# Moving a two-block transformer kernel's buffers by 64 bytes in SBUF, so that weights, 512-token and 256-token activations start at chosen multiples of 64 bytes

## What is computed

```
first_block, per layer l (trunk_layer):
    z  = (rmsnorm(x)*(1+scale)+shift) @ w_in            # 512 tokens; all columns
    y_mla, y_pool, y_gla = latent attention, pooling, gated linear attention of z
    merged = g_mla*(y_mla@w_bm) + g_pool*(y_pool@w_bp) + g_gla*(y_gla@w_bg)
    x += gate * rmsnorm(merged @ w_out, post_g)
second_block, 256 tokens:
    x += rmsnorm(attention_mixer(rmsnorm(x)));   x += rmsnorm(swiglu(rmsnorm(x)))    # D_FF = 2816
    x += rmsnorm(recurrent_mixer(rmsnorm(x)));   x += rmsnorm(swiglu(rmsnorm(x)))
```

## Time and profile before

| | |
|---|---|
| median of 3 runs | 1559.99 us |
| the runs | 1554.19, 1559.99, 2075.18 us |
| the profiled execution: time, span | 1557.29 us, 1555.5 us |
| granted clock, mean | 0.978 of full speed |
| PE busy | 1454.0 us, 93% of the span |
| DVE busy | 898.4 us, 58% |
| ACT busy | 719.7 us, 46% |
| moved by DMA, whole run | 212.56 MB, mean 137 GB/s |

### The profile page before, as it was taken

One profiled execution on the slowest core, in us unless ns is written; L12 is line 12 of the kernel. 1 busy time (PEld: TensorE's weight loads), 2 busy tenths in 40 slices (PEclk: granted clock), 3 DMA queues, 4 the chain that ended last, 5 costly groups with the idle time before them and its releaser, 6 DMA issues.

```text
span 1555.5 us, 23747 instructions
## 1 busy us (share of the span) xinstructions
PE 1454.0 (93%) x9888; PEld 1259.2 (81%) x9888; DVE 898.4 (58%) x1497; ACT 719.7 (46%) x1152; POOL 98.2 (6%) x125
## 2 busy tenths in 40 slices
PE   4999999999999997999999899989999999799997
PEld 2666666687877775777888898878999989799997
DVE  4454663534453626676366558766766558766642
ACT  4433333523325344544545545666444468644442
POOL 0200000000000020000000010001221000112100
PEclk9999999999999999999999999999999999999999
DMA  8433333122223270322254455425556626356651
GB/s 337 132 108 115 130 122 110 54 81 82 82 68 108 82 260 30 106 96 68 78 167 136 150 192 194 136 69 169 186 189 216 230 70 181 130 189 187 183 189 53
DMA packets 58841, 212.56 MB, mean 137 GB/s; under 512 B 6448, under 2 KB 7728, under 8 KB 58736
## 3 DMA queue, kind: packets, MB, share of 16 engines
q1 hardware_dynamic: 57408, 205.29, 40.0%
q0 software_dynamic: 1328, 5.77, 1.2%
HBM read 209.98 MB, written 1.05 MB: 136 GB/s over the span
## 4 chain that ended last, share of the span: by engine, by line
PE 81%; DVE 11%; ACT 5%; issue 1%; DMA 1%; SPq 1%; ACTq 0%; DVEq 0%
PE B L651 51%; PE B L669 8%; PE B L1083 7%; DVE WL L1877 3%; PE B L795 3%; ACT WH L1280 2%; PE B L1066 1%; DMA RAW<-wstream 1%; PE B L1094 1%; PE B L681 1%; PE B L875 1%; PE B L862 1%; PE B L730 1%; PE B L989 1%; PE B L1056 1%
## 5 line engine op out<-in xcount | busy, mean ns | idle before, releaser
L1877 DVE TENSOR_TENSOR WL<-RAW,WH 128x1024 fp32r<-128x1024 f32 x336 | 411.1, 1230 | 383.3 <-ACT WH L1280 382.2
L651 PE MATMUL B<-XH,WH 128*128 128x256 f32 (+1 forms) x1600 | 510.8, 319 | 4.3 <-DVE ZG L2088 2.7
L651 PE MATMUL B<-XH,WL 128*128 128x256 f32 (+1 forms) x1600 | 494.8, 309 | 0.0
L651 PE MATMUL B<-XL,WH 128*128 128x256 f32 (+1 forms) x1600 | 494.6, 309 | 0.0
L1280 ACT ACTIVATE WH<-RAW 128x1024 fp32r<-128x1024 f32 x336 | 346.5, 1052 | 111.7 <-DMA RAW<-wstream 111.5
L651 PEld LDWEIGHTS B<-XH,WH 128*128 128x128 f32 x1600 | 304.8, 190 | 31.7 <-issue 7.9
L651 PEld LDWEIGHTS B<-XL,WH 128*128 128x128 f32 x1600 | 305.0, 191 | 21.6 <-issue 6.0
L651 PEld LDWEIGHTS B<-XH,WL 128*128 128x128 f32 x1600 | 304.7, 190 | 17.1
L669 PE MATMUL B<-XH,WH 128*128 128x256 f32 (+1 forms) x208 | 73.0, 351 | 25.3 <-DVE XL L2321 13.3
L1083 PE MATMUL B<-HH,WL 128*128 128x256 f32 x304 | 85.1, 280 | 0.0
L1083 PE MATMUL B<-HL,WH 128*128 128x256 f32 x304 | 85.1, 280 | 0.0
(11 more groups left out here) (327 smaller groups left out, 2432.2 us busy)
## 6 DMA issues: line engine op xcount, KB each, us to landing
RAW<-wstream SPq DMA_DIRECT2D x384, 512.0 KB, 3.6
X<-x_t SPq DMA_DIRECT2D x4, 512.0 KB, 7.0
SW<-small POOLq DMA_DIRECT2D x2, 896.0 KB, 8.7
SW<-small POOLq DMA_DIRECT2D x2, 768.0 KB, 7.3
BT<-rel POOLq DMA_DIRECT2D x1, 1024.0 KB, 15.0
X<-consts POOLq DMA_DIRECT2D x1, 768.0 KB, 8.3
out_t<-X SPq DMA_DIRECT2D x3, 256.0 KB, 2.4
BT<-rel POOLq DMA_DIRECT2D x1, 512.0 KB, 10.5
```

The lines of the kernel that those rows point to most:

```text
L651: last = mm(out, w, x, start=i == 0, stop=i == len(pairs) - 1)
L1877: v.tensor_tensor(lo_of(h), raw_of(h), hi_of(h).bitcast(f32), ALU.subtract).then_inc(lo_ready, 1)
```

## The change

All tiles at `kb(n)` move up by 64 bytes, except those that are moving operands 256 wide. `base` is now rounded to 128, which leaves it at 16512. `o` is forced to be 64 above a multiple of 128, which it was. `even(n)` is `kb(n) + 64`. The first block's `XH`, `XL` become two tiles for its two layers, at `even` for the first and at `kb` for the second; `YH`, `YL` and `ZG` likewise.

```diff
-        base = (nc.sbuf_base + 63) // 64 * 64
+        base = (nc.sbuf_base + 2 * LINE - 1) // (2 * LINE) * 2 * LINE
...
-        o = at
+        o = at + (LINE - at) % (2 * LINE)
...
+        def even(n):
+            return kb(n) + LINE
...
-        SLOT_AT = [8 * KB_ * i for i in range(4)] + [kb(113), kb(121), kb(133), kb(141), kb(48), kb(134), kb(142), kb(16), kb(24),
...
+        SLOT_AT = [8 * KB_ * i for i in range(4)] + [even(113), even(121), even(133), even(141), even(48), even(134) + 2 * LINE,
+                                                   even(142) + 2 * LINE, even(16), even(24), even(0), even(8), even(16), even(24),
...
-        XH, XL = sb("XH", kb(0), KT, TOK, dt=f32r), sb("XL", kb(16), KT, TOK, dt=f32r)
+        XH = [sb(f"XH{l}", at, KT, TOK, dt=f32r) for l, at in enumerate((even(0), kb(0)))]
+        XL = [sb(f"XL{l}", at, KT, TOK, dt=f32r) for l, at in enumerate((even(16), kb(16)))]
...
-        YH = [sb(f"YH{l}", kb(133), 4, w, dt=f32r) for l, w in enumerate(WIDE)]
+        YH = [sb(f"YH{l}", even(133) + LINE * l, 4, w, dt=f32r) for l, w in enumerate(WIDE)]
...
-        PA = sb("PA", kb(56), 2, SEQ)
-        PB_ = sb("PB", kb(58), SEQ)
+        PA = sb("PA", even(56), 2, SEQ)
+        PB_ = sb("PB", even(58), SEQ)
...
-        aS, aA = kb(62), kb(78)
+        aS, aA = even(62), even(78) + LINE
         XH2 = sb("XH2", kb(0), KT, SEQ, dt=f32r)
         XL2 = sb("XL2", kb(8), KT, SEQ, dt=f32r)
```

More of the change, by code:

```diff
@@ L28 @@
 HALF = 8 * P
+LINE = 64
 PLAN = {}
@@ L390, in program @@
-        aS, aA = kb(62), kb(78)
+        XH = [sb(f"XH{l}", at, KT, TOK, dt=f32r) for l, at in enumerate((even(0), kb(0)))]
+        XL = [sb(f"XL{l}", at, KT, TOK, dt=f32r) for l, at in enumerate((even(16), kb(16)))]
+        XN = sb("XN", even(32), KT, TOK)
+        M0 = sb("M0", even(32), KT, TOK)
+        SQ = sb("SQ", even(56), KT, TOK)
+        PA0, PB0 = sb("PA0", even(72), 2, TOK), sb("PB0", even(76), TOK)
+        RA, RB = sb("RA", even(129), TOK), sb("RB", even(131), TOK)
+        CV = [sb(f"CV{i}", a, KT, 32) for i, a in enumerate((even(109), even(133), even(138)))]
@@ new lines, in program @@
+        MROW = [sb(f"MROW{i}", a, 512) for i, a in enumerate((even(103), even(78)))]
+        SQ3 = sb("SQ3", even(121), 3, TOK)
+        WIDE = [TOK, SEQ]
+        ZG = [sb(f"ZG{l}", (even, kb)[l](32), 12, w) for l, w in enumerate(WIDE)]
+        YL = [sb(f"YL{l}", (even, kb)[l](32), 12, w, dt=f32r) for l, w in enumerate(WIDE)]
+        YH = [sb(f"YH{l}", even(133) + LINE * l, 4, w, dt=f32r) for l, w in enumerate(WIDE)]
+        Z = sb("Z", even(56), 12, TOK)
+        VG = sb("VG", even(80), 4, 512)
@@ new lines, in program @@
+        SW = sb("SW", even(88), SW_MORE + NSW)
+        VM = sb("VM", even(142), 4, 512)
+        QB, KB = sb("QB", even(109), 4, TOK), sb("KB", even(117), 4, TOK)
+        PR, PT = sb("PR", even(105), 2, 512), sb("PT", even(125), 4, 512)
+        ROPET = sb("ROPET", even(151) + 64, SEQ)
+        CS = sb("CS", even(150), SEQ + 2 * PADW)
+        DF = sb("DF", even(151) + 64, SEQ)
+        MG = [sb(f"MG{l}", even(101), KT, w) for l, w in enumerate(WIDE)]
+        SG = [sb(f"SG{l}", even(117), KT, w) for l, w in enumerate(WIDE)]
@@ L1946, in lowered @@
                     wait(xh_ready)
-                    last = v.scalar_tensor_tensor(out=XL[:, k, s], in0=XN[:, k, s], scalar=MOD[:, 3 * KT * l + k, e:e + 1],
-                                                  in1=XH[:, k, s].bitcast(f32), op0=ALU.add, op1=ALU.subtract)
+                    last = v.scalar_tensor_tensor(out=XL[l][:, k, s], in0=XN[:, k, s], scalar=MOD[:, 3 * KT * l + k, e:e + 1],
+                                                  in1=XH[l][:, k, s].bitcast(f32), op0=ALU.add, op1=ALU.subtract)
                 last.then_inc(xl_ready, 1)
```

64 lines of the change are left out of this document (21 added, 43 removed).

## The result

| | before | after |
|---|---|---|
| median | 1560.97 us | 1551.47 us |
| profiled execution: time, span | 1557.3, 1555.5 us | 1553.2, 1551.4 us |
| PE busy | 1454.0 us | 1450.3 us |
| DVE, ACT busy | 898.4, 719.7 us | 898.2, 720.2 us |

The ratio is 0.994 (95% interval 0.992 to 0.997): 9.5 us less by the medians, 4.1 less between the two profiled executions. That is no change by the 2% bound, and inside the range forecast. The sum behind the forecast was nevertheless wrong in two of its largest terms, in opposite directions: the feed-forward stages and the 512-wide products of the first layer.

A forecast was written before the change was run, and what follows sets the result against it. PE's own pace was taken to bound the kernel. Feed-forward stages +2.0, other 256-wide -2.0, 512-wide -4.0 and L795 +0.9 sum to -3.1 us, from 1557.3 to 1554 us; range 1538 to 1561.

The forecast's parts named there:

- What bounds the kernel: Whole kernel: PE's own pace sets the time more than any wait; PE is busy 93% of the span.
- 512-wide streams want the same parity: First layer: 1392 matmuls go from different to same parity, from a mean of 230.0 to 226.7 ns; -4.0 us.
- I take even-even to be as odd-odd, since the row shows a relation between two streams: 512-wide, first layer: two even starts, seen in no row, taken at 226.7 ns; bounds -4.6 to +6.2 us.
- the slower rival: 512-wide, first layer: even-even runs at 233.3 ns, +6.2 us in place of -4.0; 1564 us in all, chance 0.08.
- A run takes its pace when it restarts: Feed-forward stages: pace is fixed at restart behind another kind of product; both taken to settle at 117.8 ns, +2.0 us.
- there is no same-parity column left to throw the run back: Feed-forward stages: all columns have different parity after, so nothing returns a slow run to the fast pace, 113.3 ns.
- The prediction's own sign of being wrong: Feed-forward stages: the forecast is wrong if they mix paces within a run, or the restart behind PB comes out fast.
- both stages fast: Feed-forward stages: both run at 113.3 ns, by a fast restart or a fall at a column border; -10.6 us, chance 0.25.
- Other 256-wide work: 256-wide matmuls outside the feed-forward stages: -3.9 us on PE, half counted as on the path, -2.0 us.
- L802, +0.9: L795 before, first layer: 192 matmuls become even-even at 120.0 ns; +0.9 us.
- The rule of the Trainium skill named ahead: PE's read ports are independent, so operand place could not change a matmul's pace; by it alone the sum is nil.

The follow-up runs named there:

- e_low_0: The changed kernel with all tiles behind the held tensors another 128 bytes up, first layer's slots 0 to 3 at distance 0: 1541.55 us, ratio 0.989.
- e_best: e_low_0 with CH, AH, HH and others moved so 256-wide products are at distance 64, slots 9 and 10 at 192: 1536.86 us, ratio 0.986.
- e_no_kick: e_best with slots 9 and 10 moved by another 128 bytes, so every 256-wide product is at distance 64: 1550.31 us, ratio 0.994.
- e_all_same: The kernel before with slots 0 to 3 and held tensors 64 bytes up, the rest placed so every distance is 0: 1573.85 us, ratio 1.009.
- m1: Program of matmuls alone, weights' start put 0 to 448 bytes past the activations': with 256 moving, 120.0 ns at distance 0, 113.3 at 64.

## Why the prediction came out as it did

**What bounds the kernel: right.** PE's pace sets the time. DVE and ACT did not move (1232 and 1054 ns against 1230 and 1052), and the pace gained in the PE-bound feed-forward stages appeared in the end.

**"512-wide streams want the same parity": wrong.** The term was -4.0 us. The first layer lost 5.9, of which L802 is 0.6 and the stretch at lower clock 1.7, which leaves some +3.6; the pace alone, 1392 matmuls from 229.8 to 232.7 ns, gives +4.0. The failing step is "I take even-even to be as odd-odd, since the row shows a relation between two streams". It is a relation, but modulo 256 bytes: in before, the same-parity pairs had distance 0, the new ones 128. The step had a price on the other side, +6.2 at 233.3 ns, and the pace came out at 232.7. So what the slower rival (chance 0.08) foresaw for slots 0 to 3 came true, though not its rule: slots 7 and 17, even-even too, kept 226.7.

**"A run takes its pace when it restarts": half right, and the term furthest off.** The first stage restarted at 117.8 as forecast. Wrong was "there is no same-parity column left to throw the run back": a change from 192 to 64 does it too. In before no 256-wide product with its weights stationary had distance 64, so its trace could not show this. The borders between whole columns that a run reached at 117.8 ns, and how many of them ended in a fall to 113.3:

| kernel | border from 192 to 64 | distance stays at 192 | stays at 64 |
|---|---|---|---|
| after | 8 of 10 | 0 of 19 | 0 of 6 |
| e_low_0 | 6 of 10 | 0 of 12 | 0 of 10 |
| e_best | 8 of 8 | 0 of 2 | 0 of 8 |
| e_no_kick | none | 0 of 5 | 0 of 75 |

So between whole columns only a change from 192 to 64 ended the slow pace, and it did not always do so. The prediction's own sign of being wrong, stages that mix paces within a run, came true twice over: by the fall at slot 11, and by the rise where `HH` takes over from `XH2`. No run shows the cause of that rise; in e_low_0 it happens with the distance unchanged. The diff did show the extra 128 bytes of slots 9 and 10 and of `HH`; parity was blind to them. The second stage restarted fast, behind a column in slot 11 at distance 64. The term was +2.0 us and came out at some -9.2 by start times; the rival "both stages fast" had -10.6.

**Other 256-wide work: -2.0 forecast, -0.7 measured.** On PE itself it gained more than forecast: outside the feed-forward stages the odd-odd matmuls went from 119.8 to 115.1 ns and the others from 115.5 to 116.0, and their gaps sum to 5.9 us less, where 3.9 had been forecast. So the wrong part is the half counted as being on the path. The attention's path goes through VectorE's low parts, as said; how much of the rest was lost to such waits and how much to the clock (0.94 against 0.96 from the first stage's end to the second) was not separated. e_all_same shows the opposite case, with most of what PE lost on the path.

**L802, +0.9: right in sign.** Its pace is 118.7 and not 120.0, since its distance is 128; the two pieces cost 0.6.

**Sum.** Forecast -3.1 us, measured -4.1 between the profiled executions: the first layer lost 5.9 where a gain of 3.1 was forecast (4.0 less L795's 0.9), and the stages gained 9.2 where a loss of 2.0 was. The number was hit by cancelling, which is luck. The range, 1538 to 1561, would have held the mistake in the stages alone (about 1543) but not the one in the 512-wide term alone (+4.0 in place of -4.0, about 1562).

The rule of the Trainium skill named ahead (SBUF — State Buffer, "Who interferes with whom": independent ports for moving operand and weight loads, PE waits for nobody) would have given no change at all. For f32r streams the measurements decide against what was drawn from it: 120.0 against 113.3 ns in m1 with nothing else running and only the weights' start moved by 64 bytes.

## What to carry to other kernels

When two groups of tiles differ in pace by place alone, list their full addresses modulo a few powers of two and ask which modulus the trace can tell apart. Here parity fitted every row and was the wrong rule, and a small program of bare matmuls would have told. Compare the granted clock too, stretch by stretch, before a difference of a few us between two executions is put down to the change. For f32r columns of this kind, lay weights and moving operand a multiple of 256 bytes apart for 512 moving, and 64 bytes apart for 256 moving. With every narrow product at 64, though, e_no_kick was no faster than the changed kernel; so check in the timeline that long runs are at the lower of the two paces, and put a change from 192 to 64 into the cycle of slots where they are not.

## What the chip showed that I had not expected

- An f32r matmul's pace depends on the distance of its operands' starts modulo 256 bytes, by up to 5.9% (113.3 to 120.0 ns) with 256 moving and 2.9% (226.7 to 233.3) with 512. The distance is not all: at 128, with 256 moving, the common address decides between 118.5 and 120.0 (m1).
- At distances 64 and 192 with 256 moving there are two stable paces, 113.3 and 117.8, both at full granted clock. One sequence in e_no_kick stayed at 117.8 for all its 1416 matmuls (granted clock 1.00 from 1090 to 1240 us).
- In the middle of a column (L1063 after, L1056 before) a plain f32 product resets the pace. At distance 192 all 13 such places in the traces came out at 117.8. At distance 64 with the weights at 128 modulo 256, the 8 that were at 113.3 ahead of it were at 117.8 behind it, and the 2 at 117.8 came out at 113.3; with the weights at 0 the 3 seen stayed fast. That the product swaps two phases is a reading, not tested.
- Where the granted clock is 0.50 (938.6 to 942 us of before) a 256-wide matmul takes 213.3 ns at distance 0 and at 192 alike: the difference by place is gone.
- Open: what in the chip repeats with 256 bytes, why a change from 192 to 64 brings a fall in most cases and not in all, and why `HH` in place of `XH2` can bring the slow pace back. The traces show start times, not what a stream waited for.
